# Expert rows gathered as four picks of 32 tokens and summed on PE's column tiles, with h2 copied four times over and a weight ring of three places

## What is computed

```python
def block_fn(hb):                      # 128 tokens
    q = (hb @ w_query).reshape(t, PEER_HEADS, 2, PEER_HALF)
    s = jnp.einsum('thpc,hpnc->thpn', q, sub_keys)
    v1, i1 = lax.top_k(s[:, :, 0], PEER_TOPK)
    v2, i2 = lax.top_k(s[:, :, 1], PEER_TOPK)
    ...
    best, pos = lax.top_k(cand, PEER_TOPK)
    experts = jnp.take_along_axis(cand_idx, pos, axis=-1)
    gate = jax.nn.softmax(best, axis=-1)
    u = expert_u[experts]
    vsel = expert_v[experts]
    act = jax.nn.gelu(jnp.einsum('thkd,td->thk', u, hb), approximate=False)
    return jnp.einsum('thk,thkd->td', gate * act, vsel)
```

## Time and profile before

| | us |
|---|---|
| three runs | 1992.1, 1992.26, 1986.85 (median 1992.1) |
| the profiled execution | 1989.17 |
| its span on the core | 1987.3 |
| PE busy | 1792.5 (90%) |
| DVE busy | 736.9 (37%) |
| ACT busy | 431.7 (22%) |
| POOL busy | 295.6 (15%) |

### The profile page before, as it was taken

How to read it: one execution, slowest core, us unless ns; L and a number is a source line. 1 busy time by engine, 2 the same in 40 slices (tenths; PEclk the granted TensorE clock), 3 DMA queues, 4 the chain that set the end, 5 groups by cost and what they waited for, 6 DMA issues and landing times.

```text
span 1987.3 us, 16408 instructions
## 1 busy us (share of the span) xinstructions
PE 1792.5 (90%) x6076; PEld 1080.0 (54%) x6076; DVE 736.9 (37%) x1743; ACT 431.7 (22%) x1173; POOL 295.6 (15%) x268
## 2 busy tenths in 40 slices
PE   6998977898898898989978989999998969999998
PEld 3444463655344443434426857688643445678853
DVE  3643167555876775766632121100001141210001
ACT  3311133223333333332321011200001031110000
POOL 0000003233453443434330000000000000000000
PEclk8998998899899999999998999999999979999999
DMA  9524328899999999999992432344434312334430
GB/s 359 204 85 170 148 96 323 341 414 417 397 422 418 411 417 402 420 407 418 397 415 101 165 132 85 127 149 147 163 112 160 136 43 102 110 127 138 158 148 21
DMA packets 139099, 467.21 MB, mean 235 GB/s; under 512 B 6240, under 2 KB 51296, under 8 KB 105616
## 3 DMA queue, kind: packets, MB, share of 16 engines
q0 software_dynamic: 37584, 270.75, 33.4%
q1 hardware_dynamic: 100720, 191.29, 27.2%
q10 hardware_dynamic: 720, 4.19, 0.6%
HBM read 465.16 MB, written 1.05 MB: 235 GB/s over the span
## 4 chain that ended last, share of the span: by engine, by line
PE 70%; DMA 15%; DVE 8%; ACT 4%; issue 2%; SPq 1%; POOL 0%; DVEq 0%; POOLq 0%; ACTq 0%
PE bank L511 23%; DMA arena<-in_peer_rows,pidx 14%; PE bank L907 11%; PE bank L544 8%; PE bank L624 6%; PE bank L555 5%; PE bank L573 4%; PE bank L699 2%; DVE arena L2039 2%; PE bank L870 2%; DMA ring<-in_w_mod 1%; PE bank L860 1%; PE bank L678 1%; SPq L440 1%; PE bank L596 1%
## 5 line engine op out<-in xcount | busy, mean ns | idle before, releaser
L511 PE MATMUL bank<-hT_all,ring 128*128 128x256 f32 x2048 | 450.6, 383 | 4.3 <-ACT hT_all L1118 3.0
L511 PEld LDWEIGHTS bank<-hT_all,ring 128*128 128x128 f32 x2048 | 393.8, 193 | 60.6 <-issue 6.0
L2039 DVE SCALAR_TENSOR_TENSOR arena<-arena,h_all 128x1024 f32<-128x1024 f32 x256 | 310.4, 1224 | 239.5 <-DMA arena<-in_peer_rows,pidx 238.3
L1545 POOL DMA_INDIRECT arena<-in_peer_rows,pidx x256 | 290.8, 1136 | 718.7 <-PE bank L907 364.6
L907 PE MATMUL bank<-arena,keep 128*128 128x512 f32 x512 | 239.7, 612 | 38.2 <-ACT keep L1399 38.2
L907 PEld LDWEIGHTS bank<-arena,keep 128*128 128x128 f32 x512 | 97.0, 195 | 167.5 <-issue 103.2
L907 PE MATMUL bank<-arena,diag 128*128 128x512 f32 x256 | 134.3, 651 | 40.1 <-ACT diag L1399 39.9
L544 PE MATMUL bank<-ring,arena 128*128 128x512 f32 x384 | 167.4, 597 | 3.1 <-DVE arena L2188 2.0
L544 PEld LDWEIGHTS bank<-ring,arena 128*128 128x128 f32 x384 | 73.0, 191 | 94.8 <-issue 89.7
L2188 DVE TENSOR_TENSOR arena<-arena,bank 128x512 f32 (+1 forms) x22 | 15.1, 688 | 294.9 <-PE bank L511 294.9
L907 PE MATMUL bank<-arena,ones 128*128 128x512 f32 x256 | 124.4, 609 | 0.0
(11 more groups left out here) (323 smaller groups left out, 1658.9 us busy)
## 6 DMA issues: line engine op xcount, KB each, us to landing
ring<-in_ffn_w_gu SPq DMA_DIRECT2D x44, 1024.0 KB
ring<-in_w_mod SPq DMA_DIRECT2D x12, 2048.0 KB
ring<-in_ffn_w_down SPq DMA_DIRECT2D x10, 2048.0 KB
ring<-in_mem_w_kv SPq DMA_DIRECT2D x8, 2048.0 KB
ring<-in_w_in SPq DMA_DIRECT2D x6, 2048.0 KB
ring<-in_conv_w_in SPq DMA_DIRECT2D x6, 2048.0 KB
ring<-in_peer_w_query SPq DMA_DIRECT2D x4, 2048.0 KB
ring<-in_mem_w_q SPq DMA_DIRECT2D x4, 2048.0 KB
```

The costliest lines, as they stand in the source:

```text
L511: m = mm(L(n, b // 2)[:, (b % 2) * TOK:(b % 2 + 1) * TOK], slot8[w][:, k, b * P:(b + 1) * P], src[:, k], start=(k == 0), stop=(k == KC - 1))
L1545: nc.gpsimd.indirect_dma_start(out=row_in[n % SLOTS], out_offset=None, in_=a["peer_rows"], in_offset=bass.IndirectOffsetOnAxis(ap=pidx[:, ...
L2039: stt(uslot[n % SLOTS], uslot[n % SLOTS], 1.0, h2[:, g // 8], ALU.mult, ALU.mult, accum_out=pact2[:, 16 * (g % 2) + k:16 * (g % 2) + k + 1 ...
```

## The change

Row n of a head is no longer pick k of 128 tokens. The 16 picks of a head are gathered as 4 x 4: gather n takes for the 32 tokens of group n % 4 four picks, on partitions 32 q to 32 q + 31 each. The number of gathers, their size and their places stay.

- To lay numbers and gates out that way, DVE `spread` masks them into 128 columns, PE `regroup` multiplies them by a matrix of ones where token numbers agree modulo 32, and DVE `select` takes each partition's own and writes pidx. Gathers wait for `rows_chosen` instead of `topk_done`.
- The dots need h2 of 32 tokens on all four quarters of the partitions: `repeat_tokens` on PE and `repeat_copy` on ACT make four such tiles `h2_rep` (16 KB per partition), for tile 0 ahead of the first dots, for tile 1 at pick 128 (there half by DVE).
- The sum: `diag` is 128 x 32, eight of them, and its product goes into 32 partitions of the bank, column tile n % 4. Two picks are issued together, half by half.
- `ring` has three places. The queries and keys of heads 2 and 3 of tile 0 move behind the output projection of tile 1. `residual_out(1)` moves ahead of all dots. PE's side work goes by a list PICK_WORK, a few entries one or two pairs of picks later or earlier; DVE does `then` ahead of `half_top` and the others; the loops over gate and up are written out, since four pieces no longer divide by the ring.

The core of the diff:

```diff
-RING = 4
+RING = 3
...
+def regroup_at(c):
+    return 16 * (c - 1) + 2
...
-        diag = [keep[:, K_COS:K_COS + P], keep[:, K_SIN:K_SIN + P], diag2[:, :], ones[:, :]]
+        diag = [keep[:, K_COS + 32 * i:K_COS + 32 * i + 32] for i in range(8)]
+        eq32, of_group = keep[:, K_EQ:K_EQ + 32], keep[:, K_OF:K_OF + 4]
+        h2g = [h2_rep[:, i * 1024:(i + 1) * 1024] for i in range(4)]
...
+            def repeat_tokens(t, g):
+                if t:
+                    pe.wait_ge(dots_done, 125 + g)
+                for half in range(2):
+                    b = open_unit(f"e{t}{g}" + "ab"[half])
+                    for q in range(4):
+                        m = mm(b[32 * q:32 * q + 32, :], ident[:, 32 * g:32 * g + 32], h2[:, t, half * 512:(half + 1) * 512], start=True, stop=True)
+                    m.then_inc(unit_ready, 1)
+            def regroup(c):
+                pe.wait_ge(sem("spread_ready"), c + 1)
+                b = open_unit(f"g{c}")
+                mm(b[:, 0:P], keep[:, K_EQ:K_EQ + P], s_all[:, c * 256:c * 256 + P], start=True, stop=True).then_inc(unit_ready, 1)
...
+            regroup(0)
+            repeat_tokens(0, 0)
+            repeat_tokens(0, 1)
             key_scores(0, 1)
-            query("q02", 2, slice(0, P))
             diff_turn(1, 2)
-            key_scores(0, 2)
+            repeat_tokens(0, 2)
+            repeat_tokens(0, 3)
...
             out_half(1, range(4, 8))
             out_half(1, range(0, 4))
+            regroup(1)
+            for h in (2, 3):
+                query(f"q0{h}", h, slice(0, P))
+                key_scores(0, h)
...
-            for n in range(16 * PK):
+            for n0 in range(0, 16 * PK, 2):
...
-                pe.wait_ge(sem("diag_ready"), n + 1)
+                pe.wait_ge(sem("diag_ready"), n0 + 2)
                 for b in range(2):
-                    m = mm(acc[b][:, :], diag[n % 4], vslot[n % SLOTS][:, b * 512:(b + 1) * 512],
-                           start=(n % 128 == 0), stop=(n % 128 == 127))
-                m.then_inc(v_used, 1)
+                    for n in (n0, n0 + 1):
+                        r = 32 * (n % 4)
+                        m = mm(acc[b][r:r + 32, :], diag[n % 8], vslot[n % SLOTS][:, b * 512:(b + 1) * 512],
+                               start=(n % 128 < 4), stop=(n % 128 >= 124))
+                        if b == 1:
+                            m.then_inc(v_used, 1)
...
+            def spread(g):
+                b = g % 4
+                dve.wait_ge(gate_exp_done, g + 1)
+                link(nc.vector.reciprocal(prz, pz4[:, b:b + 1]))
+                link(ts(comb[:, b, 1], comb[:, b, 1], prz, None, ALU.mult))
+                tt(s_all[:, g * 256:g * 256 + P].rearrange("p (g n) -> p g n", g=4), comb4[:, 32 * b:32 * b + 32].unsqueeze(1).to_broadcast([P, 4, 32]),
+                   of_group.unsqueeze(2).to_broadcast([P, 4, 32]), ALU.mult).then_inc(sem("spread_ready"), 1)
+            def select(g):
+                b = g % 4
+                own = s_all[:, g * 256 + P:(g + 1) * 256].rearrange("p (n q) -> p n q", q=4)
+                link(tt(own, unit_in(f"g{g}")[:, 0:P].rearrange("p (n q) -> p n q", q=4), of_group.unsqueeze(1).to_broadcast([P, 32, 4]), ALU.mult))
+                dve.nop().then_inc(unit_free["D"], 1)
+                nc.vector.tensor_reduce(grouped4[:, 32 * b:32 * b + 32], own, AX, ALU.add).then_inc(gate_ready, 1)
+                dve.wait_ge(gate_ready, g + 1)
+                ts(pidx[:, 16 * b:16 * b + 16].rearrange("p (m g) -> p g m", g=4), grouped[:, b, :, 0], 0.25, None, ALU.add).then_inc(sem("rows_chosen"), 1)
...
                     dve.wait_ge(rows_in[n % SLOTS], 16 * (n // SLOTS + 1))
-                    stt(uslot[n % SLOTS], uslot[n % SLOTS], 1.0, h2[:, g // 8], ALU.mult, ALU.mult,
+                    stt(uslot[n % SLOTS], uslot[n % SLOTS], 1.0, h2g[n % 4], ALU.mult, ALU.mult,
...
-            gate_scale(0)
-            gate_scale(1)
             for g in range(16):
+                if g == 8:
+                    for i in range(4):
+                        repeat_copy(1, i)
                 for q in range(4):
                     dots(g, q)
+                    for work in then.get((g, q), ()):
+                        work()
                     if q == 0 and 1 <= g <= 14:
-                        gate_scale(g + 1)
+                        select(g + 1)
```

More of the change, by code:

```diff
@@ L2021, in _ @@
             diff_max(1, 3)
+            select(0)
             key_copy(0, 1)
@@ L2033, in _ @@
             choose(1)
+            residual_out(1)
+            select(1)
             def dots(g, q):
@@ L2091, in _ @@
                             half_top(g + 2, q)
-                        else:
-                            (best_pairs if q == 2 else pair_rows)(g + 2)
-                    for work in then.get((g, q), ()):
-                        work()
+                        elif q == 2:
+                            best_pairs(g + 2)
+                        else:
+                            pair_rows(g + 2)
+                            spread(g + 2)
             add_experts(1)
```

229 lines of the change are left out of this document (143 added, 86 removed), and 6 rows, old and new, of the table UNITS.

## The result

The changed kernel takes 2055.35 us (median of 4 runs, 2054.94 to 2061.15), the kernel before, run beside it, 1991.28 us: a ratio of 1.033, 95% interval 1.031 to 1.034. It is slower by 64 us. The forecast had 2014 and a range to 2032: the direction was right, the size was not. The profiled execution took 2054.94 us, its span is 2053.1 us, 65.8 more than before.

A forecast was written before the change was run, and what follows sets the result against it. DMA was taken to bound the gathers' stage, PE the stages before and after. 26 + 4.3 - 7.3 + 0.5 = +23.5 us on 1989.2 us gave 2012.7, median put at 2014 us; range 1998 to 2032.

The forecast's parts named there:

- the ring in the first stage: Three places instead of four make PE wait for late weights ahead of the gathers: +26 us, bounds 16 and 32.
- the start of the gathers: Expert choice, h2 copies and two moved queries delay the first pairs; 20 us later shrinks to +4.3 us, bounds -1 and +14.
- the copies of pick 128: Second h2 copied at pick 128: DVE stands about 12 us while eight gathers (20 us) fill the places, +0.5 us.
- PE's cheaper pairs: Pairs of picks at 1.9 instead of 3.7 us; only idle DMA time in the gathers' stage counts: -7.3 us, bounds 0 and -13.
- the three pieces: In-projection 3, modulation piece 9 and in-projection 2 each arrive late in the first stage, PE standing 7.3 us for each.
- modulation piece 5: First-stage weight piece issued at 151.88 us, 1.2 us late, but covered by PE's 2.45 us wait for DVE.
- the forecast's 5 us: Slower PE clock after each of the three first-stage ring stalls: three times 1.7 us.
- rival 1: PE, not DMA, paces the gathers, so cheaper pairs speed the stage; if it held by a quarter, 1957 us; 5%.
- Rival 5: Slow start: modulation piece 11 and query piece 2 come late beside gathers, PE waits, places fill; +12 us, 2026 us; 10%.
- Rival 2: DVE's new wait: `select` comes before PE has caught up, holding dots of four picks; 14 heads at 2.5 us, 2048 us; 7%.
- rival 3: Ring stalls mostly hidden: two of the three early stalls meet waits already there; 1998 us; 13%.
- rival 4: Column tiles don't overlap, so pairs stay at 3.7 us and the 7.3 us stay; 2021 us; 10%.

The follow-up runs named there:

- kernel 1: Changed kernel with four weight places in the first stage, the fourth borrowed from h2_rep until its copies are written: 2019.8 us, ratio 1.0125.
- kernel 2: Kernel before the change, using only three of its four ring places until query piece 0: 2024.1 us, ratio 1.016.
- kernel 4: kernel 1 with queries 2 and 3 of the first 128 tokens moved behind picks 2 and 4: 2006.59 us, ratio 1.009.
- kernel 6: kernel 4 with the second tokens' h2 copies made at picks 94 to 110 into a ring place, first copies' place joining the ring: 2000.04 us, ratio 1.0046.
- kernel 5: Changed kernel without the four h2 copies at pick 128, second tokens' dots taken with the first tokens' h2: 2046.59 us, ratio 1.026.
- kernel 13: kernel 6 with queries 2 and 3 of the first 128 tokens behind picks 6 and 8 instead of 2 and 4: 1997.87 us, ratio 1.004.
- kernel 8: Changed kernel with expert matmuls from pick 64 on given a second time with weights of zero: 2077.3 us, ratio 1.044.
- kernel 10: Kernel before the change, with PE waiting for two picks, working half by half and freeing both places at the pair's end: 1998.94 us, ratio 1.004.
- kernel 7: Changed kernel with PE's two loops over a pair exchanged, both halves of one pick before the next: 2055.86 us.
- kernel 9: kernel 8 with each pick waited for and its place freed by itself, both halves of a pick together: 2097.63 us, ratio 1.054.

## Why the prediction was wrong

The direction was right, and the ring was rightly named as the main cost. The size was missed in each term, always to the same side. The terms as the runs give them:

| term | forecast | by the runs |
|---|---|---|
| the ring in the first stage | +26 | +35.6 (kernel 1), +32.5 (kernel 2) |
| the start of the gathers | +4.3 | +13.2 (kernel 4) |
| the copies of pick 128 | +0.5 | +6.6 (kernel 6), +8.8 (kernel 5) |
| PE's cheaper pairs, and all else | -7.3 | +8.8 (kernel 6 over the kernel before) |

The first numbers of the last column add up to 64. The last row is what is left, not something that a run measured by itself; kernel 13 takes 2.2 us off it, not clear of the spread.

**The ring, "Sum: +26 us".** The mechanism and the three pieces were right, each of the waits too small, and the step "1.2 us late, but PE waits 2.45 us for DVE ... anyway" (modulation piece 5) was wrong. Kernels 1 and 2 give 32 to 36 us. By the trace: the three waits are 7.89, 8.07 and 8.12 us instead of 7.3; modulation piece 5 came 2.90 us late and the wait for DVE behind it stayed (2.43 us at 184.91 us), as DVE had been shifted by the same stalls; query piece 0 was 1.82 us, not 0.7. The matmuls behind all three stalls are slower (29.71 for 27.63 us, 3.64 for 1.92, 8.55 for 7.03), 5.3 us together: there the forecast's 5 us were right. A stall moves PE's partners with it, so the waits on DVE and ACT that I had let absorb 1.5 us and piece 5 gave nothing back. The one that did shrink, from 3.93 to 2.43 us at 195.65 us, did so because PE's matmuls ahead of it were slower by as much. The bound of 32 was also too low.

**The start of the gathers, "+4.3 us".** This step was off by 9 us, as much as the ring, on a forecast of 4.3. Query piece 1 took 9.9 us from its issue at 357.70 us to PE's start at 367.61 us (forecast 7), and the first pair came 25 us later behind the projection than before, not 20. The count that turned 20 us into 4.3 ("the gather that went out at 370.19 us goes at 374.5") was too kind: at gather 20 the local loss was 50.3 - 36 = 14 us, the upper bound, and kernel 4 took 13.2 us back by order alone.

**Pick 128, "+0.5".** The forecast let "eight gathers (20 us) fill the places" cover DVE's 12 us. DVE stood only 8 us (749.18 to 757.17 us, copies among it), so the size of the wait was not what failed, but the cover. A full place is no help until it is free again: DVE's dots had to wait behind PE and the copies, and behind them ACT's weights and PE's pair before a place is free; POOL waited 12.7 us for PE ahead of the gather of 765.30 us. Kernels 5 and 6 give 8.8 and 6.6 us.

**PE's cheaper pairs, "-7.3".** 1.91 us per pair was right, and rival 1 was rightly put low, as a cheaper PE did not shorten the gathers' stage: from gather 8 to gather 255 it took 714.4 us before, 716.0 after, and 713.2 in kernel 13, where the hole of pick 128 is gone. The 7.3 us did not come. The step that failed is the count of idle DMA time that a faster PE would fill. Its "3 to 5 us for all the rest" was read from an average share of 0.99. But 0.01 of 752 us is 7.5 us, less than the hole (7.4 us by the earlier trace rows) and the 8 us at the end together, and shares in these views go above 1, so that they can't be read that finely (before):

```profile
380.00:1050.00 670.00, 594.74 (x1608) 294.81 (x1607) 428.39 (x1010) 220.89 (x676) 267.87 (x233) 0.97 1.01 411
```

From gather 20 on, behind the hole at the start, the stage was 668.0 us before, 680.4 after and 673.5 in kernel 13: longer, not shorter. What I also missed is the grouping. Doubling the matmuls cost 22 us (kernel 8), pairing at the old cost 8 us (kernel 10). The new order by pairs would then need the cheap matmul, and part of the gain would go to pay for it. That is a reading and not shown: why a pair of the old cost is worth 22 us in one kernel and 8 in the other was not separated. (An eighth of 230 us, in rival 1, is 29 and not 24; nothing hangs on it.)

**Rivals.** Rival 5's waits came, 4.16 us for modulation piece 11 at 447.96 us and 13.66 us for query piece 2 at 471.30 us, but not its price of 12 us: the DMA share was full from 460 to 490 us and 0.95 to 0.98 from 490 to 530 us. Rival 2's waits came too (DVE for `regroup`: 31.9 us in 10 times). Seven of them, 12.5 us together, stand in windows of 10 us whose DMA share was 0.99 or more; those that ended at 432.33 us (5.41 us), 503.63 us (10.47 us) and 765.29 us (3.47 us) stand where it was 0.70, 0.95 to 0.96 and 0.79, so they may have had a price, less than the rival's. Rivals 1, 3 and 4 did not happen.

**What stays open.** In kernel 13 gather 8 leaves at 333.23 us, 9 us later than before, because PE's first pair waits for dots that stand behind the projection, and the last gather is still 8 us late; two ways to start earlier ended in other waits. One place where its DMA rests, and that of the kernel before does not (1.02), is 450 to 460 us. PE works off a query there ahead of `regroup`, and DVE stands 10.49 us for it (PE, DVE, window):

```profile
450.74 7.59 PE L779 MATMUL bank<-hT_all,ring 128*128 128x256 f32 x32
458.16 0.38 PE L804 MATMUL bank<-s_all,keep 128*128 128x128 f32 x2
...
458.58 0.29 DVE L2115 TENSOR_TENSOR s_all<-bank,keep 128x128 f32<-128x128 f32 x1 [10.49 <-PE bank L804]
...
450.00:460.00 10.00, 10.00 (x44) 7.11 (x42) 1.20 (x6) 0.60 (x1) 1.88 (x2) 0.92 0.72 251
```

That is rival 2's mechanism, with some 3 us of resting DMA. `regroup` ahead of that query was not tried.

The tail from the convolution's first projection on, forecast unchanged, took 925.6 us against 921.1 in the profiled executions, with its waits the same to within 1.3 us. This is no loss that the change is shown to cause: kernels 2 and 10, whose tail is that of the kernel before, took 922.1 and 924.5 us, and kernel 8, which kept PE's clock up ahead of it, 925.3 us. The kernels built on the changed one lie between 922.9 and 925.7 us.

## What to carry to other kernels

A prefetch place is priced at the tightest two or three uses, and the stall there is paid in full, with the partner engines' waits moved along; don't let waits on engines that hang on the stalled one absorb anything. When memory shrinks, look for which place frees the weights that the very next step wants, and put work that needs neither between them: the order gave back 13 us at no memory. Buffers with different lifetimes (copies made late, weights needed early) can share a place, which gave back 42 us here.

## What the runs showed of the hardware

- Matmuls of 32 weight columns cost by their order only in longer runs: four took 1.91 us with neighbours in different column tiles and 1.92 us with neighbours in one (kernel 7), but eight took 3.65 us where tiles changed every second matmul and 5.36 us where they changed every fourth (kernels 8 and 9), 7.11 and 8.86 us for two such pairs behind each other.
- At full clock 16 records of this shape took 1.92 us on four column tiles and 8 records 1.91 us on two (changed kernel, 1116.04 us): the count per tile went with the time, not the count in all.
- As PE's load in the gathers' stage fell, so did its granted clock: in stretches of 50 us from 0.92 to 1.00 (400 to 1000 us, before) to 0.60 to 0.94 (400 to 1100 us, after). A pair took 3.56 us at 1111.09 us, behind 3.06 us of idle, and 1.91 us at 1116.04 us. No run changes the clock alone, so what this cost is not shown.
